# Other places in memory for the weights of a three-layer transformer on one Trainium2 core

## The reference

```python
def conv_ffn(y, w_up, conv_w, conv_b, w_down):
    up = y @ w_up
    u, v = jnp.split(up, 2, axis=-1)
    ...
    return (jax.nn.gelu(c, approximate=False) * v) @ w_down
...
    for layer in range(DEPTH):
        ...
        h = h + rms_norm(y, nw[1])
        y = conv_ffn(rms_norm(h, nw[2]), ffn_w_up[layer], ffn_conv_w[layer], ffn_conv_b[layer], ffn_w_down[layer])
        h = h + rms_norm(y, nw[3])
...
        merged = (jax.nn.sigmoid(a_m) * (merge_heads(y_m) @ w_br_moba[layer])
                  + jax.nn.sigmoid(a_f) * (merge_heads(y_f) @ w_br_fox[layer])
                  + jax.nn.sigmoid(a_c) * (merge_heads(y_c) @ w_br_mem[layer]))
        x = x + merged @ w_out[layer]
        h2 = rms_norm_2(x, g_ffn[layer])
        x = x + (jax.nn.silu(h2 @ w_gate[layer]) * (h2 @ w_up[layer])) @ w_down[layer]
```

## Time and profile before

| | us |
|---|---|
| median of 3 runs | 1096.86 |
| lowest, highest | 1093.92, 1098.75 |
| the profiled execution | 1095.88 |
| its span, first to last instruction | 1094.1 |
| tensor engine busy with matmuls | 1086.6 (99%) |
| weight loads | 959.6 (88%) |
| vector engine busy | 748.6 (68%) |
| scalar engine busy | 600.4 (55%) |
| DMA queue of the weights, share of 16 engines | 55.2% |

### The profile page before, as it was taken

The page is one execution under the profiler, slowest core; times in us unless marked ns, Lnnn a source line. Parts: engine busy times, 40 slices in busy tenths (PEclk is TensorE's granted clock), DMA queues, the critical chain, the costliest instruction groups (busy, mean ns, idle before and its releaser), DMA issues.

```text
span 1094.1 us, 16723 instructions
## 1 busy us (share of the span) xinstructions
PE 1086.6 (99%) x6712; PEld 959.6 (88%) x6712; DVE 748.6 (68%) x1109; ACT 600.4 (55%) x994; POOL 109.1 (10%) x127
## 2 busy tenths in 40 slices
PE   8999999999999999999999999999999999999998
PEld 7988989888888899898888888889999989888887
DVE  7876595998846566859788566766656885666651
ACT  6744465776734545557667445357444644555640
POOL 4020000121100000001111001121000000111100
PEclk9999999999999999999999999999999999999999
DMA  8751356666664755366566656474433555666661
GB/s 287 284 174 59 121 206 211 193 190 188 185 192 152 269 150 146 126 225 189 187 190 184 195 182 212 135 234 135 115 99 113 167 159 196 189 181 187 192 193 39
DMA packets 56957, 192.29 MB, mean 176 GB/s; under 512 B 6832, under 2 KB 9776, under 8 KB 56880
## 3 DMA queue, kind: packets, MB, share of 16 engines
q1 hardware_dynamic: 56880, 191.22, 55.2%
HBM read 190.15 MB, written 1.05 MB: 175 GB/s over the span
## 4 chain that ended last, share of the span: by engine, by line
PE 95%; DVE 2%; POOL 1%; ACT 1%; issue 0%; DMA 0%; DVEq 0%; ACTq 0%; POOLq 0%
PE ps L929 28%; PE ps L1019 19%; PE ps L1010 15%; PE ps L1020 10%; PE ps L1285 5%; PE ps L1159 3%; PE ps L1105 3%; PE ps L1082 2%; PE ps L1346 2%; PE ps L1094 1%; PE ps L1031 1%; PE ps L1144 1%; DVE lo L1485 1%; POOL hr L533 1%; PE ps L1051 1%; PE ps L1169 1%
## 5 line engine op out<-in xcount | busy, mean ns | idle before, releaser
L1485 DVE TENSOR_TENSOR lo<-raw,hi 128x1024 fp32r<-128x1024 f32 (+2 forms) x347 | 429.1, 1263 | 81.9 <-ACT hi L588 79.1
L588 ACT ACTIVATE hi<-raw 128x1024 fp32r<-128x1024 f32 (+2 forms) x347 | 347.0, 1036 | 82.2 <-DMA raw<-in_weights 75.5
L1019 PE MATMUL ps<-y_both,hi 128*128 128x512 f32 x912 | 320.8, 397 | 0.0
L1020 PE MATMUL ps<-y_both,lo 128*128 128x256 f32 x912 | 255.0, 280 | 0.0
L1019 PEld LDWEIGHTS ps<-y_both,hi 128*128 128x128 f32 x912 | 171.3, 188 | 41.5
L1020 PEld LDWEIGHTS ps<-y_both,lo 128*128 128x128 f32 x912 | 171.9, 189 | 0.0
L1010 PE MATMUL ps<-y_both,hi 128*128 128x256 f32 x912 | 167.6, 285 | 0.3 <-DVE lo L1485 0.3
L1010 PEld LDWEIGHTS ps<-y_both,hi 128*128 128x128 f32 x912 | 141.8, 191 | 1.1 <-DVE lo L1485 0.5
L1010 PE MATMUL ps<-y_both,lo 128*128 128x256 f32 x456 | 128.9, 283 | 0.0
L929 PE MATMUL ps<-hi,y_both 128*128 128x512 f32 x352 | 94.1, 382 | 2.2 <-DVE lo L1485 1.4
L929 PE MATMUL ps<-hi,h_hi 128*128 128x512 f32 x294 | 90.9, 391 | 0.0
(11 more groups left out here) (291 smaller groups left out, 1386.2 us busy)
## 6 DMA issues: line engine op xcount, KB each, us to landing
raw<-in_weights SPq DMA_DIRECT2D x331, 512.0 KB, 3.7
gain<-in_gains SPq DMA_DIRECT2D x10, 512.0 KB, 7.2
raw<-in_weights SPq DMA_DIRECT2D x8, 384.0 KB, 7.2
bias<-in_rel SPq DMA_DIRECT2D x16, 128.0 KB, 2.1
raw<-in_weights SPq DMA_DIRECT2D x8, 256.0 KB, 2.6
mem_x<-in_mem SPq DMA_DIRECT2D x2, 512.0 KB, 9.8
h<-in_x SPq DMA_DIRECT2D x2, 256.0 KB, 2.7
h<-in_x SPq DMA_DIRECT2D x1, 512.0 KB, 6.1
```

Source lines behind the costliest of these rows:

```text
L588: act.activation(hi[:, s, :w], raw[:, s, :w], ACT.Copy).then_inc(hi_done, 1)
L1019: pe.matmul(dst, hi[:, s, at], y_both[:, :, k, :], start=k == 0, stop=False)
L1020: mm = pe.matmul(dst[:, 0:S], lo[:, s, at], y_hi[:, k, :], start=False, stop=k == KD - 1)
L1485: dve.tensor_tensor(lo[:, s, :w], raw[:, s, :w], hi[:, s, :w].bitcast(F32), ALU.subtract).then_inc(lo_done, 1)
```

## The change

The two rings (`hi`, and `lo` with `raw` in the same bytes) get lengths of their own, 10480 and 10384 floats in place of 10240, and `ring()` now gives a place in floats to each unit in each of them (`AT`) in place of a slot. A unit's place modulo 128 floats (512 bytes) follows from its stage by the table `DIST`, in steps of 16 floats (64 bytes). With the longer rings `hi` itself begins 64 bytes past the residue of the others; what lies behind the rings keeps its residue, for which a few small tensors move into larger ones (`block_causal` into the still unused `mk_t`, `snk` and `esnk` into spare rows of `top` and `tot`) and the filler goes. This gives, against the residue at which all token tensors begin:

| stages | units of each | `hi` of a unit | `lo` (and `raw`) |
|---|---|---|---|
| up0, up1, up2 | 38 | 64 bytes before it | the same residue |
| odd_qk, odd_out, lead1, gates, branches, merge_out, lead2 | 16, 8, 6, 24, 12, 8, 6 | 64 bytes after it | 64 bytes before it |
| all others | | the same residue | the same residue |

`GIVER` is now the latest unit that held any byte of the new place in either ring. For 62 of the 347 units that is the unit nine before where it was ten before: 7 or 8 units in a row, 5 at the first place, around the start of up0, down0, odd_qk, up1, down1, gates, up2 and down2. The semaphores `raw_in` are taken in turn by unit number. The instructions, their order and their number on each engine stay as they are.

```diff
 LEAD, TAIL, LEADS = 6, 7, 3
+DIST = {"up0": (1, 0), "up1": (1, 0), "up2": (1, 0), "odd_qk": (7, 1), "odd_out": (7, 1), "lead1": (7, 1),
+        "gates": (7, 1), "branches": (7, 1), "merge_out": (7, 1), "lead2": (7, 1)}
+STEP, LINE = 16, 128
+LO_RING, HI_RING = RAW * UNIT + LINE + STEP, RAW * UNIT + LINE + 7 * STEP
 def ring():
-    free = [(s, -1) for s in range(FEW)]
+    kept = (RAW - FEW) * UNIT
+    names = [name for name, n, _, _ in STREAM for _ in range(n)]
+    owner = [[-1] * HI_RING, [-1] * LO_RING]
+    end, at, giver = [0, 0], [], []
     for n in range(UNITS):
-        free.append((free[n][0], n))
-        if n == last("fill") - 1:
-            free += [(s, n) for s in range(FEW, RAW)]
-    slot, giver = [x[0] for x in free[:UNITS]], [x[1] for x in free[:UNITS]]
-    return slot, giver, [slot[:n + 1].count(slot[n]) for n in range(UNITS)]
-SLOT, GIVER, TURN = ring()
+        both, last_owner = [], -1
+        for i, size in enumerate((HI_RING, LO_RING)):
+            if n < last("fill") + FEW:
+                size -= kept
+            elif n == last("fill") + FEW:
+                owner[i][size - kept:] = [last("fill") - 1] * kept
+            rest = STEP * ((7, 0)[i] - DIST.get(names[n], (0, 0))[i]) % LINE
+            p = end[i] + (rest - end[i]) % LINE
+            if p + UNIT > size:
+                p = rest
+            end[i] = p + UNIT
+            last_owner = max(last_owner, *owner[i][p:p + UNIT])
+            owner[i][p:p + UNIT] = [n] * UNIT
+            both.append(p)
+        at.append(both)
+        giver.append(last_owner)
+    return at, giver
+AT, GIVER = ring()
...
-            lo = sb("lo", [RAW, UNIT], F32R, r)
-        raw = sb("raw", [RAW, UNIT])
-        hi = sb("hi", [RAW, UNIT], F32R)
+            lo = sb("lo", [LO_RING], F32R, r)
+        raw = sb("raw", [LO_RING])
+        hi = sb("hi", [HI_RING], F32R)
...
+        block_causal = mk_t[:, 0, 0:P].bitcast(U32)
...
-        block_causal = sb("block_causal", [P], U32)
...
-        snk = sb("snk", [8, 2])
-        esnk = sb("esnk", [8, 2])
+        snk, esnk = top[:, 8:16, :], tot[:, 8:16, :]
...
-        sb("align", [88])
...
+        def hi_at(n):
+            return hi[:, AT[n][0]:AT[n][0] + UNIT]
+        def lo_at(n):
+            return lo[:, AT[n][1]:AT[n][1] + UNIT]
+        def raw_at(n):
+            return raw[:, AT[n][1]:AT[n][1] + UNIT]
...
-                    sp.wait_ge(unit_used, GIVER[n] + 1)
+                    if GIVER[n] >= 0:
+                        sp.wait_ge(unit_used, GIVER[n] + 1)
...
-                sp.dma_start(raw[:, SLOT[n], :WIDTH[n]], dram["weights"][n][:, :WIDTH[n]]).then_inc(raw_in[SLOT[n]], 16)
+                sp.dma_start(raw_at(n)[:, :WIDTH[n]], dram["weights"][n][:, :WIDTH[n]]).then_inc(raw_in[n % RAW], 16)
...
-                act.wait_ge(raw_in[s], 16 * TURN[n])
-                act.activation(hi[:, s, :w], raw[:, s, :w], ACT.Copy).then_inc(hi_done, 1)
+                act.wait_ge(raw_in[n % RAW], 16 * (n // RAW + 1))
+                act.activation(hi_at(n)[:, :w], raw_at(n)[:, :w], ACT.Copy).then_inc(hi_done, 1)
...
-                    pe.matmul(dst, hi[:, s, at], y_both[:, :, k, :], start=k == 0, stop=False)
-                    mm = pe.matmul(dst[:, 0:S], lo[:, s, at], y_hi[:, k, :], start=False, stop=k == KD - 1)
+                    pe.matmul(dst, hi_at(n)[:, at], y_both[:, :, k, :], start=k == 0, stop=False)
+                    mm = pe.matmul(dst[:, 0:S], lo_at(n)[:, at], y_hi[:, k, :], start=False, stop=k == KD - 1)
```

More of the change, by code:

```diff
@@ L778, in _ @@
                     act.activation(whole(hg), whole(hg), ACT.Silu).then_inc(hg_evac, 1)
-                    act.activation(warm[:, 8:16], half[:, 8:16], ACT.Exp)
+                    act.activation(warm[:, :], half[:, 8:16], ACT.Exp)
                 if hh in (4, 6):
@@ L785, in _ @@
             act.wait_ge(dve_sink, 1)
[L786 removed]
+            act.activation(esnk, snk, ACT.Exp).then_inc(act_sink, 1)
             even_hi(1, 1, 2)
@@ L888, in _ @@
             gate_copy(11)
-            act.activation(warm[:, 8:16], half[:, 8:16], ACT.Sigmoid)
+            act.activation(warm[:, :], half[:, 8:16], ACT.Sigmoid)
             for b in range(4):
@@ L1008, in features_of @@
                         at = slice(k * cols + f * P, k * cols + (f + 1) * P)
-                        for w, x, first, final in ((hi, yh, True, False), (hi, yl, False, False), (lo, yh, False, True)):
-                            mm = pe.matmul(dst, w[:, s, at], x(k), start=first and k == 0, stop=final and k == nk - 1)
+                        for w, x, first, final in ((hi_at, yh, True, False), (hi_at, yl, False, False), (lo_at, yh, False, True)):
+                            mm = pe.matmul(dst, w(n)[:, at], x(k), start=first and k == 0, stop=final and k == nk - 1)
                 return mm
             def features_pair(n, dst):
-                s = SLOT[n]
                 pe.wait_ge(lo_done, n + 1)
@@ L1142, in _ @@
                         k = 2 * (n - FIRST["even_i"]) + kk
-                        for x, w in ((y_hi, hi), (y_hi, lo), (y_lo, hi)):
-                            mm = pe.matmul(ps[:, 4 + t, :], x[:, k, t * P:(t + 1) * P], w[:, SLOT[n], 512 * kk:512 * kk + 512],
-                                           start=k == 0 and x is y_hi and w is hi, stop=k == KD - 1 and x is y_lo)
+                        for x, w in ((y_hi, hi_at), (y_hi, lo_at), (y_lo, hi_at)):
+                            mm = pe.matmul(ps[:, 4 + t, :], x[:, k, t * P:(t + 1) * P], w(n)[:, 512 * kk:512 * kk + 512],
+                                           start=k == 0 and x is y_hi and w is hi_at, stop=k == KD - 1 and x is y_lo)
                 mm.then_inc(unit_used, 1)
@@ L1157, in fill @@
                         wait_unit(n)
-                    for x, w in ((yh, hi), (yh, lo), (yl, hi)):
-                        mm = pe.matmul(ps[:, 6, t * 256:t * 256 + 256], x[:, k, t * P:(t + 1) * P], w[:, SLOT[n], c],
-                                       start=k == 0 and x is yh and w is hi, stop=k == KD - 1 and x is yl)
+                    for x, w in ((yh, hi_at), (yh, lo_at), (yl, hi_at)):
+                        mm = pe.matmul(ps[:, 6, t * 256:t * 256 + 256], x[:, k, t * P:(t + 1) * P], w(n)[:, c],
+                                       start=k == 0 and x is yh and w is hi_at, stop=k == KD - 1 and x is yl)
                     if t == 1 and k % 4 == 3:
@@ L1189, in even_part @@
                     wait_unit(n)
-                for x, w in ((y_hi, hi), (y_hi, lo), (y_lo, hi)):
+                for x, w in ((y_hi, hi_at), (y_hi, lo_at), (y_lo, hi_at)):
                     for c in range(2):
-                        mm = pe.matmul(ps[:, (0, 6)[t] + c, :], x[:, k, tok], w[:, SLOT[n], 512 * c:512 * c + 512],
-                                       start=u == 0 and x is y_hi and w is hi, stop=u == KD - 1 and x is y_lo)
+                        mm = pe.matmul(ps[:, (0, 6)[t] + c, :], x[:, k, tok], w(n)[:, 512 * c:512 * c + 512],
+                                       start=u == 0 and x is y_hi and w is hi_at, stop=u == KD - 1 and x is y_lo)
                 if t == 1:
@@ L1284, in lead @@
                                     k, c = 4 * half_ + kk, slice(256 * kk, 256 * kk + 256)
-                                    mm = pe.matmul(lead_place(layer, j, t), x[:, k, tok], w[:, SLOT[n], c],
+                                    mm = pe.matmul(lead_place(layer, j, t), x[:, k, tok], w(n)[:, c],
                                                    start=k == 0 and i == 0, stop=k == KD - 1 and i == 2)
@@ L1343, in out_part @@
                     wait_unit(n)
-                for x, w in ((0, hi), (0, lo), (1, hi)):
+                for x, w in ((0, hi_at), (0, lo_at), (1, hi_at)):
                     for c in range(2):
-                        mm = pe.matmul(ps[:, (6, 0)[t] + c, :], out_y(x, k // 4, tok)[:, k % 4, :], w[:, SLOT[n], 512 * c:512 * c + 512],
-                                       start=k == 0 and x == 0 and w is hi, stop=k == KD - 1 and x == 1)
+                        mm = pe.matmul(ps[:, (6, 0)[t] + c, :], out_y(x, k // 4, tok)[:, k % 4, :], w(n)[:, 512 * c:512 * c + 512],
+                                       start=k == 0 and x == 0 and w is hi_at, stop=k == KD - 1 and x == 1)
                 if t == 1:
```

44 lines of the change are left out of this document (22 added, 22 removed).

## The result

| | before | after |
|---|---|---|
| median, us (4 runs each) | 1097.80 | 1079.36 |
| all runs, us | 1093.92 to 1098.86 | 1078.73 to 1079.80 |
| ratio of after to before | | 0.9831, 95% interval 0.9817 to 0.9844 |
| profiled execution | 1095.88 | 1079.69 |
| its span | 1094.1 | 1077.9 |

The account below looks back on a forecast made before the run. The prediction took the spacing of the tensor engine's matmuls as the bound. Terms -10.2 - 4.1 + 0 + 0.7 = -13.6 us took the profiled 1095.88 to 1082.3; with the median 1.0 over, 1083.3 us, 8-in-10 range 1067 to 1108.

Parts of the forecast that it names:

- What bounds the kernel: Tensor engine busy 1086.6 of 1094.1 us; next to no waiting left, so only faster succession of matmuls can pay.
- 13.3 ns is not a fixed price: Each float32r matmul's time over its columns: about 2.5 ns real change-over, 11 of two streams colliding, which distance could alter.
- Matmuls of 256 columns: odd_qk, gates, branches, both leads: 1536 matmuls win one quantum of 6.67 ns each, -10.2 us; bounds 15.4 won, 10.2 lost.
- The up pairs: up1 and up2 come to up0's price, up0 keeps it: -4.1 us; bounds 23.7 won, 6.1 lost.
- 512 columns in odd_out and merge_out: 192 matmuls in two stages: taken as 0, between 2.1 us won and 1.3 us lost.
- Later loads: 62 units wait for one unit more, some 2.8 us: +0.7 us; bounds nothing and 22 us at eight places.
- DVE and ACT at other distances: Reads and writes of both engines at new distances: 0 while DVE has 11% of slack; 14 us if that cover went.
- No effect: Rival 1: the 13.3 ns is the float32r matmul's own and distance does nothing; 1098 us, chance 0.23.
- Slower by a common residue being the good place: Rival 2: matmuls at a new distance cost one quantum more, 17.6 us over 2640; 1115 us, chance 0.17 in whole or part.
- All of it: Rival 3: the streams come free altogether, -40.5 us; 1056 us, chance 0.12.
- The ring: Rival 4: distances do little and loads come late at several places, 5 to 10 us of waits; 1102 to 1107, chance 0.05.
- The signs: What would show it: branches 27.2 us, leads' 60 in 6.8, three up1 pairs 1.04, down1 57.2; opposite-signed gains would refute.

Follow-up runs that it names:

- s1: The changed kernel's rings with another table, each of fourteen stages given its own pair of distances, such as (1,1) in lead2 and merge_out; 1102 us.
- g9: The changed kernel with three units (204 to 206, the first behind down1) waiting for one unit more; 1088.51 us, 9.1 more than the changed kernel.
- a_zero: The changed kernel with the table of distances emptied, so new rings but all operands at the common residue; 1097.81 us, ratio 0.9999 to before.
- a_up: The changed kernel with distances kept for the three up stages alone, (1,0); 1085.43 us, ratio 0.9892 to the kernel before.
- a_rest: The changed kernel with distances (7,1) kept for the other seven stages alone, up stages at the common residue; 1089.02 us, ratio 0.9923 to before.
- p4: The changed kernel with every distance that isn't nought enlarged by four steps, 256 bytes: up (5,4), the other seven (3,5); 1079.69 us, ratio 0.9846 to before.

## Why the prediction was right, and where its terms were not

- **What bounds the kernel**: right. Only the spacing of the matmuls changed; DVE, ACT and the loads gave no wait of note.
- **13.3 ns is not a fixed price but two streams in each other's way, in quanta of 6.67 ns**: right in that distance changes it, and by a quantum in branches and the up stages. Elsewhere the means are no whole quanta (leads 117.7, 512 columns 230.0, a pair at (0.5,0) 344.7). Not shown is the picture behind it, that the moving stream passes the weight load. It was an inference from plain float32 and remains one.
- **Matmuls of 256 columns**, -10.2 us: measured -7.1 (odd_qk, gates, branches and both leads). The step that failed is the count. Branches gave the full quantum (120.0 to 113.4). In gates and odd_qk the mean fell by 4.9 and 5.2 ns; in gates 0.4 us of longer wait for `lo` is in this, without which it is 5.7 ns. An eighth and a fifth of their distances stay at 115 ns or above; why these do is open. And the leads gave 2.2 ns in place of 6.67: there the weights stream, and (7,1) isn't their best pair; `s1` had 114.1 ns at (1,1). I had put both forms under one price.
- **The up pairs**, -4.1 us: measured -10.1. The chosen value was the low price that up0 already showed; (1,0) is a quantum below that in all three stages, 340 ns. The bound of 325 was not reached by any pair of distances tried.
- **512 columns in odd_out and merge_out**, 0: measured +0.4, within the bounds and on the losing side.
- **Later loads**, +0.7: right for this table, with about 0.5 us of more waits beside those in even_a. (At down1 nine units in a row had the later giver, not 7 or 8.) But the upper bound was priced wrongly: a late unit costs next to nothing at the 62 places of this table and 9.1 us at the one of `g9`, not 2.8 anywhere.
- **DVE and ACT at other distances**, 0: right, 1262 against 1263 ns.
- **The own time**: I took the profiled execution, 1095.88, as 1 us under the median, a matter of chance. It had up0 in the low state. By the medians 18.4 us are saved, not 16.2; that the rest is the states, which the changed kernel doesn't show, fits their 2.0 us a stage and is argued.
- **The sum**, -13.6 us: measured -16.2 between the profiles. That it came so near is partly luck: the 256-column term was 3.1 us too large, the up term 6.0 too small, and the 1.1 us that the start of the program lost in this trace belong to neither.
- **The rivals.** No effect falls with `a_zero` against `a_up` and `a_rest`. By what the Trainium skill ("SBUF — State Buffer", Who interferes with whom) states of the tensor engine's two read ports, that they are independent, the distance would do nothing: 113.4 against 120.0 and 226.9 against 233.4 ns for the same matmuls at other distances don't agree with that, and the measurement decides. Whether the ports are where the effect arises no run here shows. Slower by a common residue being the good place is true of 512 columns alone, of the forms tried. All of it: no stage of 256 columns came under 113 ns. The ring, as above.
- **The signs.** Branches at 27.2 us and down1 at 57.2 came as named, three pairs in 1.02 us where 1.04 was named, the leads' 60 at 7.06, not 6.8. What I named as proof against me, opposite signs of the two gains, didn't come; but `s1` shows that it would have proved little, since one distance helps one form and hurts another: at (1,1) its lead2 won 0.9 us and its merge_out lost 0.6.

## What to carry to other kernels

When the tensor engine is busy all the time and its matmuls still stand 10 to 30 ns over their columns, look at the addresses: measure the spacing at several distances of the stationary to the moving operand modulo 256 bytes, for each form of matmul apart, since the best for one is a loss for another. One kernel with another distance in each stage measures a dozen in one trace; measure each more than once, since the same distance can have two spacings. And when a ring's places are changed, look at the unit that an engine needs ahead of a hand-over between stages: in `g9` a later load there cost 9 us, while 62 later loads elsewhere cost about half a microsecond.

## What the runs showed of the hardware

- The spacing of float32r matmuls depends on the distance between stationary and moving operand modulo 256 bytes: 113.4 to 120.0 ns for 256 columns in branches, 226.7 to 233.4 for 512, 340 to 353.6 for a pair. Moving all tensors by 64 bytes together (`shift`, one run) left branches at 120.0 and the up stages at the two spacings that nought has.
- The same instructions at the same distances can settle in one of two steady patterns, 346.7 or 353.3 ns a pair, for 296 pairs and 100 us: both stand in the one trace of the kernel before. The choice falls behind the twelve transposes, not at the start of the stage. That it also falls differently from one execution of a kernel to another is argued from run times, 2 us apart. At (1,0) only one pattern was seen, in all up stages of five kernels (`p4` with (5,4) counted), and the spread of the runs fell from 4.9 us to 1.1.
- The fill stage, whose memory tokens lie in the spare end of the rings and so came to a new distance by the longer rings alone, won 0.3 us in every kernel with the new rings, `a_zero` too. The prediction had not seen it.
